# Expert rows turned by 32x32 block transposes on VectorE, overflow loads issued earlier, one state buffer per sample

## The reference, cut to what matters

```python
def gla_recurrent(q, k, v, log_a, S0):          # for the 8 samples, one step each
    S = jnp.exp(gt)[..., None] * S + kt[..., :, None] * vt[..., None, :]   # 4 heads, 128 x 256
    o = jnp.einsum('bhd,bhdv->bhv', qt, S)

def routed_experts(x, eidx, wsel, w_gate, w_up, w_down):
    ...                                          # tokens sorted by expert, in blocks
    out = swiglu(x[toks], w_gate[e], w_up[e], w_down[e]) * wr[:, None]
    y = y.at[toks].add(out)
```

## Time and profile before

| what | us |
|---|---|
| median of 3 runs | 2013.16 |
| lowest, highest run | 2002.44, 2019.08 |
| the profiled execution's own time | 2008.22 |
| its span, from the first to the last instruction | 2006.1 |
| PE busy (74%) | 1490.3 |
| DVE busy (26%) | 521.7 |
| ACT busy (13%) | 263.6 |
| POOL busy (16%) | 325.7 |
| L1189, `gu` matmuls, 4288 of them | 498.6 |
| L1177, turning of gathered rows, 552 of them | 85.2 |
| idle time of PE ended by the landing of gathered rows | 86.0 |

### The profile page before, as it was taken

How to read it: one execution, slowest core, us unless ns; L and a number is a source line. 1 busy time by engine, 2 the same in 40 slices (tenths; PEclk the granted TensorE clock), 3 DMA queues, 4 the chain that set the end, 5 groups by cost and what they waited for, 6 DMA issues and landing times.

```text
span 2006.1 us, 26677 instructions
## 1 busy us (share of the span) xinstructions
PE 1490.3 (74%) x10124; PEld 946.0 (47%) x10124; DVE 521.7 (26%) x1394; ACT 263.6 (13%) x605; POOL 325.7 (16%) x493
## 2 busy tenths in 40 slices
PE   6998877688888777777248957866888878877742
PEld 4776565444444444444136636654444444444422
DVE  3123344211111111110442863264111111111136
ACT  1211011111111111111002123011111111111100
POOL 0002100012122222222101250000222222222210
PEclk8999688799899999999669978867999999999985
DMA  9846335989999999997660420252999999999852
GB/s 365 328 158 221 123 145 190 384 338 405 414 413 417 416 415 410 410 411 287 234 220 1 128 85 11 71 208 101 409 407 406 417 413 411 416 417 417 354 221 106
DMA packets 152780, 586.85 MB, mean 293 GB/s; under 512 B 27867, under 2 KB 45097, under 8 KB 117398
## 3 DMA queue, kind: packets, MB, share of 16 engines
q1 hardware_dynamic: 120562, 513.82, 64.4%
q0 software_dynamic: 25824, 52.00, 7.3%
q10 hardware_dynamic: 6340, 20.30, 2.7%
HBM read 578.99 MB, written 43.72 MB: 310 GB/s over the span
## 4 chain that ended last, share of the span: by engine, by line
DMA 35%; PE 34%; DVE 10%; issue 6%; ACT 3%; POOL 2%; SPq 1%; POOLq 1%; ACTq 1%; DVEq 0%
DMA arena<-h_rows,arena 17%; DMA ring<-in_moe_w_down 15%; PE PS L1199 7%; PE PS L1189 4%; PE PS L1177 3%; PE PS L757 3%; PE PS L1695 2%; PE PS L1101 2%; DMA arena<-y_rows 1%; PE PS L436 1%; PE PS L1699 1%; DVE arena L1365 1%; DVE arena L1406 1%; PE PS L1085 1%; POOL y_rows L1492 1%
## 5 line engine op out<-in xcount | busy, mean ns | idle before, releaser
L1189 PE MATMUL PS<-ring,arena 128*64 128x256 f32 x4288 | 498.6, 386 | 71.7 <-DMA ring<-in_moe_w_down 61.3
L1189 PEld LDWEIGHTS PS<-ring,arena 128*64 128x64 f32 x4288 | 332.6, 140 | 289.6 <-issue 175.2
L1199 PE MATMUL PS<-ring,arena 128*64 128x512 f32 x1072 | 284.9, 656 | 47.8 <-ACT arena L1445 47.8
L1492 POOL DMA_INDIRECT y_rows<-arena x134 | 133.9, 999 | 812.6 <-DVE arena L1365 699.3
L1365 DVE COPY arena<-PS 128x512 f32<-128x512 f32 x134 | 92.7, 691 | 483.8 <-PE PS L1199 483.8
L1361 DVE TENSOR_TENSOR arena<-arena,PS 128x128 f32<-128x128 f32 x134 | 38.5, 288 | 517.1 <-ACT arena L1443 517.1
L1177 PE MATMUL PS<-cst,arena 128*128 128x128 f32 x552 | 85.2, 302 | 86.0 <-DMA arena<-h_rows,arena 86.0
L1199 PEld LDWEIGHTS PS<-ring,arena 128*64 128x64 f32 x1072 | 69.6, 145 | 165.5 <-issue 87.7
L1443 ACT ACTIVATE arena<-PS 128x128 f32<-128x128 f32 x134 | 37.2, 278 | 788.9 <-PE PS L1189 788.9
L1177 PEld LDWEIGHTS PS<-cst,arena 128*128 128x128 f32 x552 | 71.2, 196 | 114.1 <-issue 114.1
L604 PE MATMUL PS<-hT,ring 128*128 128x264 f32 x384 | 88.5, 388 | 0.3 <-DVE modT L472 0.3
(11 more groups left out here) (464 smaller groups left out, 1405.4 us busy)
## 6 DMA issues: line engine op xcount, KB each, us to landing
ring<-in_moe_w_gate SPq DMA_DIRECT2D x134, 1024.0 KB, 10.0
ring<-in_moe_w_up SPq DMA_DIRECT2D x134, 1024.0 KB, 12.5
ring<-in_moe_w_down SPq DMA_DIRECT2D x134, 1024.0 KB, 17.4
ring<-in_w_ada SPq DMA_DIRECT2D x32, 1152.0 KB, 11.8
arena<-y_rows ACTq DMA_DIRECT2D x8, 2048.0 KB, 7.6
ring<-in_w_ada SPq DMA_DIRECT2D x16, 768.0 KB, 14.0
ring<-in_gla_w_in SPq DMA_DIRECT2D x8, 1152.0 KB, 12.8
ring<-in_dsa_w_in SPq DMA_DIRECT2D x6, 1024.0 KB, 15.3
```

What stands on the lines that cost most here:

```text
L1189: m = pe.matmul(PS[64 * half:64 * half + 64, 2 + b, 0:256].rearrange("p (g n) -> p g n", g=2), xgT[:, k, CAP * b:CAP * b + CAP], gu[:, :, ...
L1199: m = pe.matmul(PS[64 * j:64 * j + 64, 6 + b, :], hTt[b][:, kk * CAP:(kk + 1) * CAP], ring[:, s, 2, kk * D + 512 * j:kk * D + 512 * j + 51 ...
L1492: pool.indirect_dma_start(out=y_d[l], out_offset=IndirectOffsetOnAxis(ap=si[:, b:b + 1], axis=0), in_=ysb[b], in_offset=None, bounds_check ...
```

## The change

It has three parts. The turning of gathered rows goes from PE and ACT to DVE: 16 block transposes for each pair, each of 32 partitions by 256 elements, in four quarters of four. `xgT` has two buffers. For the 64 experts, DVE does quarters 0 and 1 of pair m + 1 behind `hm` of the first expert of pair m, and quarters 2 and 3 behind `hm` of the second, in both cases ahead of the copy `ysb`; quarter 0 waits for the gather. For overflow pairs it does all 16 behind `hm` of the second expert. Pair 0 is turned ahead of the first expert. POOL's gather waits for `xgT` where it waited for `tx`. The first two overflow loads are issued as soon as slots 0 and 1 have been used for the last time by the 64 experts (`y` of expert 60 and of 61), and the expert's number is read ahead of the wait. The eight states have eight buffers; those of samples 4 to 7 are loaded at once after the prompt part of GLA, ahead of all stores.

```diff
@@ -558,8 +558,8 @@
         wg1 = spare[:, TOK:TOK + P].rearrange("p (k n) -> p k n", k=KT)
         wg2 = flat(dL)[:, 0:hk]
 
-        NS = 4
-        sbuf = [arena[:, o:o + 1024].rearrange("p (h v) -> p h v", h=GH) for o in (0, 1024, 8 * TOK, 8 * TOK + 1024)]
+        NS = DEC
+        sbuf = [arena[:, o:o + 1024].rearrange("p (h v) -> p h v", h=GH) for o in (0, 1024, 8 * TOK, 8 * TOK + 1024, 6336 + 1024, 12480, 13504, 14528)]
 
 
         GP = {'g1': 0, 'z': 1, 'v_T': 2, 'kd_T': 4, 'att': 6, 'kv8_T': 8}
@@ -937,40 +937,36 @@
                     ac(act.activation(on[2], PS[:, 0, 0:GDV], ACT.Square, accum_out=oms[:, 0:1]))
                     act.activation(oms[:, 0:1], oms[:, 0:1], ACT.Sqrt, bias=K["eps"], scale=1 / GDV).then_inc(S("o_rms"), 1)
                 act.wait_ge(S("on_ready"), T + 1)
-            for i in range(NS):
-                act.wait_ge(S(f"sstate_out{i}"), 16 * len(range(i, DEC, NS)))
+            act.wait_ge(S("sstate_out"), 16 * DEC)
             act.wait_ge(S("out_pool"), 16)
 
         def pool_gla():
 
             pool.wait_ge(S("gla_dve"), GD["kmask"] + 1)
-            for b in range(NS):
+            for b in range(4):
                 pool.dma_start(sbuf[b], ins["state_gla"][0, b].rearrange("h d v -> d h v")).then_inc(S(f"sstate_in{b}"), 16)
             pool.wait_ge(S("proj_act"), 8)
             for v in range(2):
                 ins_ = pool.tensor_scalar(pT[:, 16 + v:24:2, :], pT[:, 16 + v:24:2, :], vT[:, 40 + v:41 + v], None, ALU.mult)
             ins_.then_inc(S("r_scaled"), 1)
             pool.wait_ge(S("state"), 4)
+            pool.wait_ge(S("across"), 3)
+            for b in range(4, DEC):
+                pool.dma_start(sbuf[b], ins["state_gla"][0, b].rearrange("h d v -> d h v")).then_inc(S(f"sstate_in{b}"), 16)
             pool.dma_start(outs["gla_p"][0, 0].rearrange("h d v -> d h v"), Sst[1]).then_inc(S("out_pool"), 16)
-            for b in range(NS, DEC):
-                store_state(b - NS)
-                pool.wait_ge(S(f"sstate_out{b % NS}"), 16 * (b // NS))
-                pool.wait_ge(S("so"), b - NS + 1)
-                pool.dma_start(sbuf[b % NS], ins["state_gla"][0, b].rearrange("h d v -> d h v")).then_inc(S(f"sstate_in{b % NS}"), 16)
-            for b in range(DEC - NS, DEC):
+            for b in range(DEC):
                 store_state(b)
-            for i in range(NS):
-                pool.wait_ge(S(f"sstate_out{i}"), 16 * len(range(i, DEC, NS)))
+            pool.wait_ge(S("sstate_out"), 16 * DEC)
 
         def store_state(b):
             pool.wait_ge(S("sstate"), b + 1)
-            pool.dma_start(outs["gla_s"][0, b].rearrange("h d v -> d h v"), sbuf[b % NS]).then_inc(S(f"sstate_out{b % NS}"), 16)
+            pool.dma_start(outs["gla_s"][0, b].rearrange("h d v -> d h v"), sbuf[b % NS]).then_inc(S("sstate_out"), 16)
 
 
 
         tk = carver()
         xg = tk(D)
-        xgT = tk(KT, P)
+        xgT = [tk(KT, P), arena[:, 4096:4096 + KT * P].rearrange("p (k c) -> p k c", k=KT)]
         sg = [tk(P) for _ in range(2)]
         hm = [tk(P) for _ in range(2)]
         hTt = [tk(P) for _ in range(2)]
@@ -1070,10 +1066,14 @@
                     load_expert(s, i * WS + u, l, S(f"slot_loaded{s}"))
             sp.wait_ge(S("lists"), PER["lists"] * l + 1)
             n2 = sp.value_load(npr[0:1, 0:1], min_val=1, max_val=NOV // 2)
-            with sp.Fori(0, n2) as i:
+            for u in range(2):
+                e = sp.value_load(eid[0:1, u:u + 1], min_val=0, max_val=NE - 1)
+                sp.wait_ge(M(l, "y"), NE - WS + u + 1)
+                load_expert(it_ex[l][u][0], e, l, M(l, f"over_loaded{u}"))
+            with sp.Fori(1, n2) as i:
                 for u in range(2):
+                    e = sp.value_load(eid[0:1, ds(i * 2 + u, 1)], min_val=0, max_val=NE - 1)
                     sp.wait_ge(M(l, "y"), i * 2 + (NE + u - 1))
-                    e = sp.value_load(eid[0:1, ds(i * 2 + u, 1)], min_val=0, max_val=NE - 1)
                     load_expert(it_ex[l][u][0], e, l, M(l, f"over_loaded{u}"))
 
 
@@ -1169,15 +1169,7 @@
                 pe_ada(1, [7])
                 pe.wait_ge(S("mod_T"), 16)
 
-        def pe_turn_pair(l, m):
-
-            wait_alone(pe, M(l, "gathered"), m * 16 + 16)
-            xv = xg.rearrange("t (p k) -> t k p", k=KT)
-            for k in range(KT):
-                ins_ = pe.transpose(PS[:, k // 4, (k % 4) * P:(k % 4 + 1) * P], xv[:, k, :], K["ident"])
-            ins_.then_inc(M(l, "tx"), 1)
-
-        def pe_body(l, n, h2, u, s, wsem, wval):
+        def pe_body(l, n, h2, u, s, wsem, wval, over):
 
             b = u % 2
             if b == 0:
@@ -1186,11 +1178,9 @@
             gu = ring[:, s, 0:2, :].rearrange("p g (k n) -> p g k n", k=KT)
             for k in range(KT):
                 for half in range(2):
-                    m = pe.matmul(PS[64 * half:64 * half + 64, 2 + b, 0:256].rearrange("p (g n) -> p g n", g=2), xgT[:, k, CAP * b:CAP * b + CAP],
+                    m = pe.matmul(PS[64 * half:64 * half + 64, 2 + b, 0:256].rearrange("p (g n) -> p g n", g=2), xgT[0 if over else u // 2][:, k, CAP * b:CAP * b + CAP],
                                   gu[:, :, k, half * P:(half + 1) * P], start=(k == 0), stop=(k == KT - 1), skip_group_check=True)
             m.then_inc(M(l, "gu"), 1)
-            if b == 1:
-                pe_turn_pair(l, h2 + 1)
             pe.wait_ge(M(l, "hm"), n + 1)
             pe.transpose(PS[:, 4 + b, 0:P], hm[b], K["ident"]).then_inc(M(l, "th"), 1)
             pe.wait_ge(M(l, "hT"), n + 1)
@@ -1221,10 +1211,9 @@
             def body(i, n, h2, u, over):
                 s, first = it_ex[l][u]
                 if over:
-                    pe_body(l, n, h2, u, s, M(l, f"over_loaded{u}"), i * 48 + 48)
+                    pe_body(l, n, h2, u, s, M(l, f"over_loaded{u}"), i * 48 + 48, over)
                 else:
-                    pe_body(l, n, h2, u, s, S(f"slot_loaded{s}"), i * 48 + 48 * first)
-            pe_turn_pair(l, 0)
+                    pe_body(l, n, h2, u, s, S(f"slot_loaded{s}"), i * 48 + 48 * first, over)
             main_and_overflow(pe, l, body)
 
         def pe_combine(l):
@@ -1354,11 +1343,28 @@
             if l == 0:
                 dve_ada(1, [6, 7])
 
+        def dve_turn_rows(l, m, into, quarters):
+
+            if 0 in quarters:
+                wait_alone(dve, M(l, "gathered"), m * 16 + 16)
+            for a in quarters:
+                for c in range(4):
+                    ins_ = dve.transpose(xgT[into][32 * c:32 * c + 32, :, 32 * a:32 * a + 32],
+                                         xg[32 * a:32 * a + 32, 256 * c:256 * c + 256].rearrange("t (p k) -> t k p", k=KT))
+            if 3 in quarters:
+                ins_.then_inc(M(l, "xgT"), 1)
+
         def dve_experts(l):
+            dve_turn_rows(l, 0, 0, range(4))
+
             def body(i, n, h2, u, over):
                 b = u % 2
                 dve.wait_ge(M(l, "sg"), n + 1)
                 dve.tensor_tensor(hm[b], sg[b], PS[:, 2 + b, P:2 * P], ALU.mult).then_inc(M(l, "hm"), 1)
+                if not over:
+                    dve_turn_rows(l, h2 + 1, 1 - u // 2, (0, 1) if b == 0 else (2, 3))
+                elif b == 1:
+                    dve_turn_rows(l, h2 + 1, 0, range(4))
                 dve.wait_ge(M(l, "y"), n + 1)
                 if not isinstance(n, int) or n >= 2:
                     dve.wait_ge(M(l, f"scattered{b}"), h2 * 16)
@@ -1443,13 +1449,6 @@
                 act.activation(sg[b], PS[:, 2 + b, 0:P], ACT.Silu).then_inc(M(l, "sg"), 1)
                 act.wait_ge(M(l, "th"), n + 1)
                 act.copy(hTt[b], PS[:, 4 + b, 0:P]).then_inc(M(l, "hT"), 1)
-                if b == 1:
-                    evict_pair(h2 + 1)
-
-            def evict_pair(m):
-                act.wait_ge(M(l, "tx"), m + 1)
-                act.copy(xgT.rearrange("p k c -> p (k c)"), PS[:, 0:2, :].rearrange("p b n -> p (b n)")).then_inc(M(l, "xgT"), 1)
-            evict_pair(0)
             n2 = main_and_overflow(act, l, body)
             act.wait_ge(M(l, "xgT"), n2 + (NE // 2 + 1))
 
@@ -1482,7 +1481,7 @@
             def body(i, n, h2, u, over):
                 b = u % 2
                 if b == 0:
-                    wait_alone(pool, M(l, "tx"), h2 + 1)
+                    wait_alone(pool, M(l, "xgT"), h2 + 1)
                     gather(h2 + 1)
                 if not isinstance(n, int) or n >= 2:
                     wait_alone(pool, M(l, f"scattered{b}"), h2 * 16)
```

## The result

| | median us | lowest to highest |
|---|---|---|
| before | 2010.64 | 2002.44 to 2019.08 |
| after | 2394.88 | 2391.23 to 2396.30 |

The ratio is 1.1909 [1.1871, 1.1947]. The direction was forecast, the size was not: 2107 with a range to 2190. The loss is about four times the 96 us that the sum gave.

A forecast was written before the change was run, and what follows sets the result against it. The prediction took full DMA engines in the expert stages as the bound, a gather loop just below. Terms +99 (pairs), +6.4 (starts), -4.0 (overflow), -5.6 (states) summed to +96 us; forecast 2107 us, range 2000 to 2190.

The forecast's parts named there:

- the new loop: Expert pairs: gather, transposes, `ysb`, `hm`, transposes, `ysb`, POOL take 18.1 us against 16.45, +99 us over 62 pairs.
- L: Time from a gather's issue to its landing, in the expert loop; taken as 6.9 us, 8.1 with the rings full.
- T8: Time of eight DVE transposes, twice in each pair's loop; taken as 3.2 us.
- rival 2: Transposes reading `xg` with a step of 8 elements cost more: eight take 4.5 us, 2283 us in all; chance 0.15.
- Both rows used as bounds: Trace rows bounding eight transposes: 2.67 us as one-input and 3.23 us as two-input instructions of 256 elements.
- starts: Before each layer's first `gu`, sixteen transposes take 6.4 plus 0.2 us, uncovered: +3.2 us a layer, +6.4 in all.
- overflow, layer 0: Two overflow pairs: second pair's loads go out 4.7 us earlier, last turning costs 3.7 us more: -1.0 us.
- overflow, layer 1: One overflow pair: 20.4 us from `ysb` of expert 63 to the last `ysb` becomes 17.4: -3.0 us.
- states: With all states loaded early, sample 7's update comes at 220.3 instead of 225.99: -5.6 us.
- The clock: PE stands some 4 us a pair; `th` to `y` at the lower level loses about 1 us, outside the sum.
- Rival 1: Gather landing time falls until a pair takes 16.45 us again; loop costs nothing, 2005 to 2010 us; chance 0.25.
- Rival 3: Loop holds and DMA engines run evener, 417 GB/s instead of 412: 1992 to 1997 us; chance 0.08.

The follow-up runs named there:

- experiments 6 and 8: 6: changed kernel with dense reads and two gather buffers, 1.0076. 8: kernel before with early overflow loads, eight states, two gather buffers, PE turning, 0.9953.
- the probes: Groups of eight DVE instructions added at the end of the kernel before; eight transposes took 2.72 us dense, 4.23 strided, 5.09 strided with output moving between quadrants.
- experiment 2: Kernel before with early overflow loads and eight state buffers, turning left on PE and ACT: 2020.28 us, ratio 0.9938.
- experiments 11 and 12: Kernel before with one small part each: only the eight state buffers, ratio 0.9962; only the early overflow loads, ratio 0.9985.
- experiment 10: Changed kernel with 12 extra PE products, result unused, ahead of PE's wait for the second `hm`: 2360.96 us, ratio 1.1607.

## Why the prediction was wrong

**What held.** The bound of the loop before (experiments 6 and 8), the new loop and its order, the engines that wait in it. L was taken as 6.9 and the median landing is 7.1. Everything in the loop beside T8 (the time of eight transposes) came within some tenths: 7.1 + 0.1 + 5.1 + 0.73 + 0.32 + 5.2 + 3.6 = 22.2, and 22.32 was measured.

**The step that failed: "I take 3.2 us for eight (T8) and 6.4 for sixteen."** T8 is 5.1 and sixteen take 10.2. Twice 1.9 to 2.0 is 3.9 of the 4.2 us by which a pair is longer than the 18.1 of the forecast. There were two errors in one number, by the probes:
- 1.5 us is the step of 8 elements (4.23 against 2.72). The prediction had it as rival 2, from the row of 98 elements 4 apart, and put it second, since a transpose has one input and the strided cast, with one input, paid nothing. The probe shows that a copy pays less than a two-input instruction but does pay (1.70 to 2.46), and that a transpose pays as much as a two-input instruction does. The row's 0.65 ns an element is near the measured 0.73 (1.5 us over eight times 256).
- 0.86 us is the change of partitions from one instruction to the next. Both rows used as bounds run on all 128 partitions, so they could not show it. The third, 3.57, worked out "without overlap" and set aside for 3.2, is the dense value of the loop (3.58). Its premise was the right one: in the probe, instructions that change quadrants do not overlap.

Neither bound reached the measured 5.1 alone. Both together would have come near: 3.57 without overlap, and 8 x 0.17 = 1.4 for the step, is 4.9. Rival 2, at 2283, was right in kind and also too low.

**The sum, against the trace** (layer 0 and 1, us):

| term | forecast | traces |
|---|---|---|
| 62 pairs | +99 | 62 x (22.32 - 16.46) = +363 |
| starts | +6.4 | 2 x 7.2 = +14.4 |
| overflow, layer 0 | -1.0 | 39.8 to 47.1: +7.3 |
| overflow, layer 1 | -3.0 | 20.4 to 23.6: +3.2 |
| states | -5.6 | -5.6 to -7.7 |
| last scatter, layer 1 | none | from the last copy to the end 70.7 to 72.7: +2.0 |
| sum | +96 | +382 to +384; spans differ by 388 |

**Start.** The chain of waits in the changed kernel, beside the earlier trace rows:

```profile
377.90 8.70 DMA arena<-h_rows,arena
386.73 0.62 DVE arena L1352
...
396.32 0.65 DVE arena L1352
397.20 5.75 PE PS L1181 x32
```

From the first transpose to `gu` 10.5 us, where PE's turning needed 3.24. One transpose takes 622 to 633 ns here, though the DMA engines are idle from 390 on, and 616 to 640 over the whole run: it is not contention with the loads. Layer 1's start shows the same 10.5 and 3.24 us.

**Overflow.** The waits for weights went as forecast, but sixteen transposes took their place. Layer 0, beside the earlier trace rows:

```profile
1120.46 10.25 DVE L1352 STREAM_TRANSPOSE arena<-arena 32x256 f32<-32x256 f32 x16
1130.74 0.69 DVE L1371 COPY arena<-PS 128x512 f32<-128x512 f32 x1
...
1130.95 5.80 PE L1181 MATMUL PS<-ring,arena 128*64 128x256 f32 x32 [7.78 <-DVE arena L1352]
```

Where PE turns (experiment 2), the same early loads shorten this stretch by 4.5 us in layer 0 and 4.4 in layer 1 (20.4 to 16.0); with 10.2 us of transposes behind each second `hm` both become losses. The two unused loads of layer 1 (experiments 11 and 12) were in no term of the forecast; in the changed kernel they come with the +2.0 in the table.

**States.** Right. Sample 7's update comes 2.98 us behind sample 6's, ended by PE and no longer by its load:

```profile
215.85 1.66 DVE L902 SCALAR_TENSOR_TENSOR arena<-arena,eg,PS 128x256 f32<-128x256 f32 x4 [1.32 <-PE PS L729]
218.83 1.66 DVE L902 SCALAR_TENSOR_TENSOR arena<-arena,eg,PS 128x256 f32<-128x256 f32 x4 [1.32 <-PE PS L729]
```

**The clock** stood in the upper end of the range alone. In the changed kernel it is worth about 60 us (experiment 10), by way of the gather's landing as far as the rows show, a path that no step of the prediction had; with dense reads it is 71 us, by way of `y`.

**The other rivals.** Rival 1 had L falling until the DMA engines were full. L did fall, from 8.1 to 7.1, and stayed there. Rival 3 needed rival 1.

**What it shows about the change.** Two causes act together: T8 stands twice in the loop, and the loop holds the gather because there is one `xg`. A second buffer alone takes the ratio to 1.033, dense reads alone to 1.130, both to 1.008. With the turning left on PE it is 0.994.

## What to carry to other kernels

Work that moves from an engine whose time is hidden to one that stands in a loop of waits costs its whole duration, as often as it stands in the loop, here twice in each pair; look for a second buffer before looking for a faster instruction. Price an operation that the trace lacks from rows that share its access pattern and its partitions; a row on 128 partitions with dense operands says little of many short instructions that change partitions and read with a step. Ends of a range that come from separate reasons add up where both can hold.

## What was not expected of the hardware

- Successive DVE instructions on different quadrants of partitions do not overlap, where those on one quadrant do: eight transposes of 32 x 256 take 3.58 us instead of 2.72, eight copies 2.37 instead of 1.70.
- Eight transposes that read with a step of 16 or 32 bytes take 4.2 us instead of 2.72; a step of 8 bytes is free.
- A gather of 128 rows of 4 KB issued 5.1 us or more behind a 3 MB load was used 4.9 to 6.6 us later, one issued nearer behind a load 6.7 to 8.3 us later (29 gathers of experiment 10).
- A scatter into `y_rows` landed 6.76 us after its issue where a load of 3 MB had been issued 1.4 us ahead of it, and 2.16 us after it with no load near.
- PE's granted clock in the expert window was 0.81 in the changed kernel, and 1.00 or 0.98 with useless products in its waits, at a gain of 60 to 71 us.
